# Two-block transformer kernel, first MoE: token rows fetched from DRAM by index and transposed, in place of a gather by matmul

## The reference, cut to what matters

```python
xf = h.reshape(b * t, d)                 # normed x, 256 x 1024
g_sel = argmax(xf @ w_rg + b_rg)         # one of 4 groups of 8 experts
top_v, top_i = lax.top_k(e_in_group, 2)  # two experts within the group
top_w = softmax(top_v) * g_w
combine = ...                            # 256 x 32, two non-zero weights in a row
for e in range(32):
    hid = silu(xf @ w_gate[e]) * (xf @ w_up[e])            # 1024 -> 128
    y = y + combine[:, e:e + 1] * (hid @ w_down[e])        # 128 -> 1024
```

## Time and profile before

| | |
|---|---|
| runs of the kernel before (us) | 1004.64, 997.33, 998.43; median 998.43 |
| the profiled execution: its time, its span (us) | 1000.59, 998.8 |
| PE busy, share of the span | 836.7 us, 84% |
| DVE, ACT, POOL busy | 244.0, 162.9, 56.1 us |
| moved by DMA | 307.33 MB, mean 308 GB/s |
| the chain that ended last | PE 61%, DMA 33% |

### The profile page before, as it was taken

The page is one execution under the profiler, slowest core; times in us unless marked ns, Lnnn a source line. Parts: engine busy times, 40 slices in busy tenths (PEclk is TensorE's granted clock), DMA queues, the critical chain, the costliest instruction groups (busy, mean ns, idle before and its releaser), DMA issues.

```text
span 998.8 us, 20766 instructions
## 1 busy us (share of the span) xinstructions
PE 836.7 (84%) x9275; PEld 579.0 (58%) x9275; DVE 244.0 (24%) x624; ACT 162.9 (16%) x347; POOL 56.1 (6%) x62
## 2 busy tenths in 40 slices
PE   7999999999899998999999888756657676676665
PEld 4656588885666674445665666544535454454543
DVE  2023830232422222135344412110202011020201
ACT  2012322330311114101553200000000000000000
POOL 8000300000011000061000000000000000000000
PEclk9999999999999999999799999888988888797977
DMA  9965524048478999244254899999999999999996
GB/s 255 380 218 216 209 107 169 1 184 321 169 275 323 410 402 381 97 160 168 85 204 156 323 422 413 429 430 425 427 428 430 430 427 427 427 430 430 428 427 262
DMA packets 53674, 307.33 MB, mean 308 GB/s; under 512 B 4584, under 2 KB 5824, under 8 KB 41344
## 3 DMA queue, kind: packets, MB, share of 16 engines
q1 hardware_dynamic: 50688, 301.85, 75.3%
q0 software_dynamic: 1760, 2.77, 1.1%
q10 hardware_dynamic: 1184, 2.10, 0.5%
HBM read 303.56 MB, written 3.15 MB: 307 GB/s over the span
## 4 chain that ended last, share of the span: by engine, by line
PE 61%; DMA 33%; DVE 2%; issue 1%; ACT 1%; SPq 0%; ACTq 0%; DVEq 0%
PE ps L1514 58%; DMA ring<-in_w_up 21%; DMA ring<-in_w_down 7%; DMA ring<-in_w_gate 5%; PE ps L1540 1%; DMA ring<-in_w_in 1%; PE ps L1680 1%; PE ps L1643 0%; PE ps L1568 0%; PE ps L1885 0%; ACT arena L814 0%; DVE xx L1285 0%; PE ps L1717 0%; PE ps L1829 0%; DVE arena L1236 0%
## 5 line engine op out<-in xcount | busy, mean ns | idle before, releaser
L1514 PE MATMUL ps<-ring,arena 128*32 128x128 f32 (+3 forms) x5968 | 288.1, 339 | 136.9 <-DMA ring<-in_w_gate 45.8
L1514 PEld LDWEIGHTS ps<-ring,arena 128*32 128x32 f32 (+1 forms) x5968 | 202.1, 125 | 221.4 <-issue 78.1
L1514 PE MATMUL ps<-ring,xx 128*128 128x512 f32 (+2 forms) x384 | 151.6, 553 | 0.0
L1514 PE MATMUL ps<-arena 32*128 32x256 f32 (+10 forms) x1216 | 130.8, 376 | 3.5 <-ACT arena L816 0.9
L1514 PEld LDWEIGHTS ps<-ring,xx 128*128 128x128 f32 x384 | 70.4, 192 | 75.7 <-issue 74.8
L1514 PEld LDWEIGHTS ps<-arena 32*128 32x128 f32 (+4 forms) x1216 | 82.6, 175 | 33.0 <-issue 25.4
L804 ACT ACTIVATE arena<-ps 128x128 f32<-128x128 f32 x40 | 11.1, 278 | 469.9 <-PE ps L1514 469.9
L1229 DVE TENSOR_TENSOR arena<-arena,ps 128x128 f32<-128x128 f32 x40 | 11.5, 288 | 293.6 <-ACT arena L804 293.6
L1514 PE MATMUL ps<-xx,ring 128*128 128x256 f32 (+2 forms) x400 | 78.9, 381 | 0.0
L1514 PEld LDWEIGHTS ps<-xx,ring 128*128 128x128 f32 (+2 forms) x400 | 63.6, 174 | 12.3 <-issue 1.5
L1514 PE MATMUL ps<-arena,xs 128*128 128x128 f32 x512 | 65.0, 288 | 1.9 <-DVE arena L1124 1.9
(11 more groups left out here) (266 smaller groups left out, 534.8 us busy)
## 6 DMA issues: line engine op xcount, KB each, us to landing
ring<-in_w_up SPq DMA_DIRECT2D x38, 2048.0 KB, 25.2
ring<-in_w_down SPq DMA_DIRECT2D x38, 2048.0 KB, 23.8
ring<-in_w_gate SPq DMA_DIRECT2D x37, 2048.0 KB, 23.6
ring<-in_w_in SPq DMA_DIRECT2D x15, 2048.0 KB, 18.5
ring<-in_w_out SPq DMA_DIRECT2D x4, 2048.0 KB, 8.0
arena<-in_w_gate SPq DMA_DIRECT2D x2, 2048.0 KB, 10.5
arena<-in_w_up SPq DMA_DIRECT2D x2, 2048.0 KB, 14.1
arena<-in_w_down SPq DMA_DIRECT2D x2, 2048.0 KB, 9.6
```

The costliest lines, as they stand in the source:

```text
L1514: ins = pe.matmul(dst, w, x, start=start, stop=stop, skip_group_check=True)
```

## The change: from the third group on, rows by indirect DMA

- ACT writes the normed x (`xs`, two tiles of 512 KB) to a new DRAM array, `normed_x_scratch`, as soon as it is computed.
- Groups 0 and 1 gather as before, with two `pick` buffers now in place of one. DVE writes `pick` of group n + 2 during group n, right behind the two multiplications by the gains.
- In each group n, 0 to 7, PE multiplies that `pick` by a column of token numbers (`slot_tokens`, two matmuls of one column, between the gate strips and the up strips). The result is the token number of each of the 128 slots of group n + 2. DVE copies it as an integer into `token`, behind `hidden`.
- POOL waits for it (`s_tok`) and issues an indirect DMA: 128 rows of 4 KB, the rows of `normed_x_scratch` that `token` names, into one of two buffers `xg_tm`. It does so eight times; the last two fetch the rows for groups 8 and 9, which only a further round would use. POOL's loads of `const2` and the clearing of `aug_l` and `aug_r` stand behind this loop.
- In groups 2 to 7 PE does not gather; it waits for the rows (`s_row`) and transposes them, eight transposes of 128 x 128, into the same banks.
- Ahead of the last scatter PE waits until all eight indirect DMAs have landed, since their buffers are used anew behind it.
- The semaphore of the weighted picks is a new one (`s_pw`), and PE's down strips now also wait for `s_tok`.

```diff
+        picks = [pick, kb3(15, TT, P)]
+        xg_tm = [kb(16, D), kb(20, D)]
...
+        xs_dram = nc.dram_tensor("normed_x_scratch", (T, D), F32).ap()
...
+            with pool.Fori(0, rounds) as r:
+                with pool.Fori(0, NGRP // 2) as g:
+                    for half in range(2):
+                        pool.wait_ge(s_tok, pool.snap(r * NGRP + g * 2 + (half + 1)))
+                        pool.sem_inc(s_seen, 1)
+                        pool.wait_ge(s_xd, 32)
+                        pool.indirect_dma_start(xg_tm[half], None, xs_dram,
+                                                bass.IndirectOffsetOnAxis(token[:, half:half + 1], 0)
+                                                ).then_inc(s_row[half], 16)
+                pool.wait_ge(s_rounds, 1)
+                pool.reg_load(rounds, nround[0:1, 0:1])
+
             pool.wait_ge(s_y[0], 2)
             pool.dma_start(const2, a["shape_const2"]).then_inc(s_const2, 16)
...
+                if m == 1:
+                    for tt in range(TT):
+                        act.wait_ge(s_xs, 3 + tt)
+                        act.dma_start(xs_dram[tt * P:(tt + 1) * P, :], xs[:, tt, :]).then_inc(s_xd, 16)
...
+                if b == 0:
+                    pick_slots(0, EG, 1)
...
-                def group(n, r, c_next):
+                def group(n, r, c_next, half):
                     gathered(n)
+                    dve.wait_ge(s_posm[0], dve.snap(r + 1))
+                    dve.wait_ge(s_pw, dve.snap(n + 1))
+                    pick_slots(0, dve.snap(c_next + EG), half)
                     hidden(dve.snap(n + 1), 0)
-                    next_picks(n, r, c_next)
+                    dve.tensor_copy(token[:, half:half + 1], bank(7, 1, T)).then_inc(s_tok, 1)
+                    dve.wait_ge(s_ptp[0], dve.snap(n + 1))
+                    weigh_slots(0, c_next, dve.snap(n + 2), 1 - half)
...
+                def gathered_rows(half, q):
+
+                    pe.wait_ge(s_row[half], pe.snap(q * 16))
+                    for k in range(KD):
+                        ins = pe.transpose(bank(6 + k // 4, P, (k % 4) * P), xg_tm[half][:, k * P:(k + 1) * P], ident)
...
+                def slot_tokens(n, half):
+
+                    pe.wait_ge(s_pick[0], val(n + 3))
+                    for tt in range(TT):
+                        mm(bank(7, 1, T), picks[half][:, tt, :], const[:, C_TOK + tt:C_TOK + tt + 1], tt == 0,
+                           tt == TT - 1)
...
-                    gather(n)
-                    pe.wait_ge(s_pick[0], val(n * 2 + 2))
+                    if isinstance(n, int):
+                        gather(n)
+                    else:
+                        gathered_rows(parity, q)
+                    pe.wait_ge(s_pw, n1)
...
                     for i in range(2):
                         arrived(c[i], q)
                         w4 = slot4(c[i])
+                        if i == 1:
+                            slot_tokens(n, parity)
...
                     arrived(c[2], q)
+                    pe.wait_ge(s_tok, n1)
                     pe.wait_ge(s_hid[0], n1)
...
                 if b == 0:
+                    for half in range(2):
+                        pe.wait_ge(s_row[half], pe.snap(pe.snap(rounds) * (16 * TURNS1)))
                     scatter(pe.snap(pe.snap(rounds) * NGRP + 1), last=True)
```

More of the change, by code:

```diff
@@ L142, in program @@
         stat = sb("stat", [P, 256])
-        posm = sb("posm", [P, TT, NE + EG])
+        posm = sb("posm", [P, TT, NE + 2 * EG])
+        token = sb("token", [P, 2], I32)
         comb = sb("comb", [P, TT, NE + EG])
@@ L329, in program @@
         s_pick = [sem(f"moe_picks{b}") for b in (0, 1)]
+        s_pw = sem("moe1_picks_weighed")
+        s_xd = sem("normed_x_in_dram")
+        s_tok = sem("slot_tokens")
+        s_seen = sem("slot_tokens_seen_by_pool")
+        s_row = [sem(f"slot_rows_loaded{i}") for i in (0, 1)]
         s_xgp = [sem(f"moe_gathered{b}") for b in (0, 1)]
@@ L1118, in group_columns, with pick_slots, weigh_slots @@
                 return slice(c0, c0 + EG) if isinstance(c0, int) else bass.ds(c0, EG)
-            def pick_slots(b, c0):
+            def pick_slots(b, c0, i=0):
                 shape = [P, TT, EG, SLOTS]
                 iota = const[:, C_IOTA:C_IOTA + SLOTS].unsqueeze(1).unsqueeze(1).broadcast_to(shape)
-                dve.tensor_tensor(pick.rearrange("p t (j s) -> p t j s", j=EG),
+                dve.tensor_tensor(picks[i].rearrange("p t (j s) -> p t j s", j=EG),
                                   posm[:, :, group_columns(c0)].unsqueeze(3).broadcast_to(shape), iota,
                                   ALU.is_equal).then_inc(s_pick[b], 1)
-            def weigh_slots(b, c0, picked):
+            def weigh_slots(b, c0, picked, i=0):
                 dve.wait_ge(s_pick[b], picked)
@@ L1142, in weigh_slots @@
                 dve.tensor_tensor(pick_w.rearrange("p t (j s) -> p t j s", j=EG),
-                                  pick.rearrange("p t (j s) -> p t j s", j=EG),
+                                  picks[i].rearrange("p t (j s) -> p t j s", j=EG),
                                   comb[:, :, group_columns(c0)].unsqueeze(3).broadcast_to(shape),
-                                  ALU.mult).then_inc(s_pick[b], 1)
+                                  ALU.mult).then_inc(s_pw, 1)
             def clear_route(b):
@@ L1274, in moe @@
                             for half in range(2):
-                                group(dve.snap(r * NGRP + g * 2 + half), r, dve.snap(g * (2 * EG) + (half + 1) * EG))
+                                group(dve.snap(r * NGRP + g * 2 + half), r, dve.snap(g * (2 * EG) + (half + 1) * EG),
+                                      half)
                         else:
                             group2(dve.snap(r * NGRP + g), r, dve.snap(g * EG + EG))
-                    dve.wait_ge(s_pick[b], dve.snap(r * (2 * NGRP) + (2 * NGRP + 2)))
+                    if b == 0:
+                        dve.wait_ge(s_pick[0], dve.snap(r * NGRP + (NGRP + 2)))
+                    else:
+                        dve.wait_ge(s_pick[1], dve.snap(r * (2 * NGRP) + (2 * NGRP + 2)))
                     dve.tensor_scalar(posm[:, :, :], posm[:, :, :], -float(SLOTS), None,
@@ L1805, in strips @@
                     return ins
+                def gathered_rows(half, q):
+                    pe.wait_ge(s_row[half], pe.snap(q * 16))
+                    for k in range(KD):
+                        ins = pe.transpose(bank(6 + k // 4, P, (k % 4) * P), xg_tm[half][:, k * P:(k + 1) * P], ident)
+                        if read[0]:
+                            ins.then_inc(s_used, read[0])
+                            read[0] = 0
+                        if k % 4 == 3:
+                            ins.then_inc(s_xgp[0], 1)
+                def slot_tokens(n, half):
[3 more added lines that the diff above has]
+                           tt == TT - 1)
                 def gather(n):
[L1809 removed]
+                    pe.wait_ge(s_pick[b], val(n + 1 if b == 0 else n * 2 + 1))
                     for half in range(2):
@@ L1813, in gather, with group @@
                             for tt in range(TT):
-                                ins = mm(bank(6 + half, P, i * P), xs[:, tt, k * P:(k + 1) * P], pick[:, tt, :],
+                                ins = mm(bank(6 + half, P, i * P), xs[:, tt, k * P:(k + 1) * P],
+                                         picks[n if b == 0 else 0][:, tt, :],
                                          tt == 0, tt == TT - 1)
                         ins.then_inc(s_xgp[b], 1)
-                def group(n, c, q):
+                def group(n, c, q, parity):
                     n1 = val(n + 1)
@@ L1910, in moe @@
                 if b == 0:
-                    group(0, FIRST1[0:3], 0)
-                    group(1, FIRST1[3:6], 0)
+                    group(0, FIRST1[0:3], 0, 0)
+                    group(1, FIRST1[3:6], 0, 1)
                 else:
@@ L1920, in moe @@
                             for half in range(2):
-                                group(pe.snap(r * NGRP + g * 2 + half), [s0 + 3 * half + n for n in range(3)], q)
+                                group(pe.snap(r * NGRP + g * 2 + half), [s0 + 3 * half + n for n in range(3)], q,
+                                      half)
                         else:
```

11 lines of the change are left out of this document (7 added, 4 removed).

## The result

| | before | after |
|---|---|---|
| median of 20 runs (us) | 1000.73 (997.33 to 1006.54) | 1006.88 (996.36 to 1014.04) |
| the profiled execution: its time, its span (us) | 1000.59, 998.8 | 1006.36, 1004.5 |

The ratio is 1.0051, interval [1.003, 1.0072]: the kernel is 5 to 6 us slower. The ratio goes by the fast runs and leaves out after's three slowest (1012.52 to 1014.04 us), while the medians take all twenty. The loss is less than the 1% I called the limit of no change, but the sign is wrong, and 1006.88 lies 1.9 us above my range of 991 to 1005. The forecast was 997.

A forecast was written before the change was run, and what follows sets the result against it. PE sets the first MoE's pace, with DMA weight loads close behind. PE's -17.0 + 7.2 us, less 7.6 taken back by late weights and 0.6 by the last rows, gives -1.6: 997 us from the median, range 991 to 1005.

The forecast's parts named there:

- the last rows: Before the last scatter: PE waits 0.6 us for fetched rows nobody reads; the scatter starts at 377.7 us.
- L: An indirect DMA's time from issue to landing, taken as 4.7 us for the last one; the gain is 6.3 - L.
- the first rival: Before the last scatter: the last rows land late, slower than before from 6.3 us to landing on; chance 0.28.
- a rival at 0.10: PE, waiting for weights, is granted its lower clock; costs 1 to 3 us in or behind the last group: 999; chance 0.10.
- the forecast stretch: First MoE, from the first gather's start to the last scatter's end: forecast 113.4 us, 115.04 before.
- PE, gather and token numbers: PE, first MoE: transposes replacing gathers save 17.0 us over six groups; token matmuls cost 7.2 over eight.
- The weights: SP's queue: starts 1.0 us earlier, five fetches add 6.4; last down weights at 374.3 us, taking back 7.6 of PE's gain.
- The down strips: PE, group 7: start as their weights land, 2.25 us earlier than before.
- The last scatter: PE, end of the first MoE: starts at 377.7 us instead of 379.34, with no slowing counted.
- three signs: Wrong if PE never waits for weights in groups 5-7, rows are waited for inside the loop, or 380 us gain vanishes by 550.
- The order of POOL: POOL: `const2`, clearing and small loads move behind the eighth fetch, done at about 385 us, cover over 30 us; costs nothing.
- The rival on bandwidth: Weight loads, first MoE: a second queue lets DMA reach 427 GB/s, gaining 2.7 us more, 994; chance 0.14.

The follow-up runs named there:

- quarter_rows: The changed kernel with each indirect fetch bringing 1 KB of each row instead of 4, reread by the transposes (another product): 995.26 us, ratio 0.9938.
- six_groups_const2_early: The changed kernel without the two spare fetches, with `const2`, the clearing and the small loads behind the second fetch: 1001.33 us, ratio 0.9997 against before.
- busy_wait: The changed kernel with 16 unused matmuls on PE ahead of its wait for the last rows: 1004.01 us, ratio 1.0027 against before.
- rows_in_four_groups: The changed kernel with fetched rows only in groups 2 to 5, no spare fetches, groups 6 and 7 gathering as before: 997.35 us, ratio 0.9973 against before.
- the two best: The changed kernel with rows in groups 2 to 4, or 2 to 5, `const2` behind the second fetch: 994.94 and 995.41 us, ratios 0.9952 and 0.995.
- before_again: The kernel before with only the loaded number of rounds held at 1 or more, run for a second trace: 1002.53 us, ratio 1.0012.
- no_spare_rows: The changed kernel without the fetches for groups 8 and 9 and the wait for them: 1000.17 us, ratio 1.0002 against before.
- two_groups: The changed kernel with fetched rows only in groups 2 and 3, `const2` and the small loads behind both fetches: 1000.49 us, ratio 0.9972 against before.
- four_groups_const2_early: The changed kernel with rows only in groups 2 to 5, no spare fetches, `const2` and small loads behind the second fetch: 995.41 us, ratio 0.995 against before.

## Why the prediction was wrong, by its own steps

The failed step is the last rows: "I take L = 4.7 ... The wait is 0.6 us". L was 7.0 us, and the wait 4.05. The gain was 6.3 - L by my own formula, so the deciding point was passed. I had this as the first rival, with 0.28. By that formula, though, L = 7.0 loses 0.7 us, and the stretch lost 5.0. The larger part is a second term, PE's lower clock behind a wait, which the sum had at nothing and a rival at 0.10: it cost 1.5 us in the last up strips and 2.5 in the last scatter. Of the 6.6 us between the forecast stretch and the measured one, L has 2.3, the clock 4.0.

1. **PE, gather and token numbers: right.** Eight transposes take 1.09 us (1.0). A group with all its weights takes 11.8 us (11.9). The token matmuls cost 0.67 (0.9): 0.61 of their own less what they overlap, gate and up strips together 4.37 instead of 3.70.
2. **The weights: right.** The last down weights, forecast at 374.3 us with the MoE at 267.97, thus at 380.5 with it at 274.19, landed at 380.4; the up weights at 375.3 (375.4). From the issue of group 4's gate weights to this landing it takes 72.1 us, 65.4 before: 6.7 us for five fetches, where a quarter of a load each gave 6.4. The size held; that it is all bytes, quarter_rows doesn't bear out. Also right was that the late weights take back most of PE's gain: PE idles 6.8 us for up weights in groups 6 and 7, each time longer than the 0.5 to 2.5 us I gave.
3. **The down strips: 1.5 us late.** I had them start as their weights land, 380.5. They start at 382.08, as the up strips ahead of them took 3.46 us instead of 1.95, at a granted clock of 0.60. I had put the lower clock at 0.10, said it would be hidden where weights bind, and left it out of the sum. In group 6 it is hidden: those 1.5 us only shorten the next wait. In group 7 the strips lie on the path. six_groups_const2_early has them at 1.96, and its down strips come with the weights.
4. **The last rows: failed.** They are asked for at 380.81 instead of 379.2, which is step 3 again and 0.1 more. L is 7.0, 2.3 more than I took. I had taken it from a plain load of the same size, with another behind it, and called it near since no indirect one had been seen. quarter_rows shows what that overlooks: with a quarter of the bytes the last fetch still takes 5.6 us. The second fetch of after shows it too: beside engines busy to 0.68 it took 5.4 us (4.3 in quarter_rows), where the plain load in an idle stretch took 3.4. The rest of L goes with the full engines: there whole rows took 7.0 to 8.3 us, more than the 1.28 us I had added. No run has a plain load alone in that place; `const2`, right behind the last fetch, took 8.8 us. So how much of L is owed to the rows being chosen by index stays open.
5. **The last scatter: not in the sum.** PE had idled 4.05 us, and the scatter took 6.21 us, 2.5 more than before. busy_wait shows this as the clock's, and as coming from the wait ahead of it.

From the forecast stretch, 113.4 us: +1.6 (asked for later), +2.3 (L), +0.2 (from the landing to the scatter), +2.5 (the slow scatter) gives 120.0; measured 120.07. Taking the last two fetches out and leaving `const2` early gives 112.67, 7.4 us less, and 0.7 us better than my forecast with a 0.6 us wait in it. The time of that kernel isn't below before's, though: 1001.33 us, ratio 0.9997 [0.9974, 1.002]. rows_in_four_groups has the same stretch, 112.69, and 0.9973 [0.9951, 0.9995]. So a gain of 2.4 us of stretch is at the edge of what these times show; the 4.1 and 4.2 us of the two best stand clear in both.

My range had a slip as well: its upper end of 1005 was to stand for an L near 11 us, but 6.3 - 11 gives a loss of 4.7 us and 1003.

Of the three signs that were to make the prediction wrong two didn't come: PE waited for weights in groups 6 and 7, and no rows were waited for inside the loop. The third, a gain at 380 us that is gone at 550, can't be read, as there was no gain. The profiled loss does shrink: after is 11.3 us late at the end of the last scatter, 7.9 at the second MoE's first gather and 5.7 at the end. The order of POOL, costed at nothing for the changed kernel, was costed rightly there; its ACT line 950, behind the wait, ran at 434.46 us, 160.3 from t0 (153.9 before), so with time to spare. The rival on bandwidth had nothing for it: 409 and 410 GB/s, as before.

The late start of the MoE in after, 6.22 us, lies wholly in the first block. By the matmuls that start at 103.26 us before and at 109.49 in after all of it is there, and PE's rows keep that distance up to t0; so ACT's new issues, at the MoE's start, have no part in it. Two pieces of PE's work show where more than half of it comes from, in before, then in after:

```profile
37.85 17.57 PE L1514 MATMUL ps<-ring,xx 128*128 128x8 f32 x64
...
87.88 14.00 PE L1514 MATMUL ps<-ring,xx 128*128 128x512 f32 x32
```

```profile
40.69 19.27 PE L1553 MATMUL ps<-ring,xx 128*128 128x8 f32 x64
...
92.41 15.70 PE L1553 MATMUL ps<-ring,xx 128*128 128x512 f32 x32
```

```profile
45.00:50.00 5.00, 5.00 (x9) 1.97 (x8) 0.51 (x2) 0.06 (x1) 0.00 (x0) 0.66 1.05 387
90.00:95.00 5.00, 5.00 (x14) 2.65 (x13) 1.64 (x6) 2.72 (x4) 0.00 (x0) 0.78 0.49 158
```

After is 2.84 us late before the first pair, in the first projection, and before_again is by 3.1 in the same place; each of the two stretches at a granted clock of 0.66 and 0.78, where before has 1.00, adds 1.70. What stays open is what starts these two stretches. Seven of the ten traces of kernels made from the changed one have them, the two of before don't, nor do no_spare_rows (which starts with before_again: 271.07, 271.04), two_groups and four_groups_const2_early. So they aren't tied to the change as such; that it makes them more likely is neither shown nor ruled out.

## What to carry to other kernels

A transfer that nobody reads still has a price if something waits for it, and most of all at the end of a stage, where no later work covers its time to landing; leave it out or move the wait. When a change makes an engine wait, price the wait and also the slower work right behind it: 1.1 to 2.7 us here for waits of 2.2 to 4.1 us. Once two resources are near their limit, shifting all of the work from one to the other turns the bound round: without spare rows and with `const2` early, six groups took 2.4 us off the stretch, three or four groups 4.2 and 4.1 us.

## What the runs showed of the hardware

- An indirect fetch of 128 rows of 4 KB takes POOL 0.94 to 1.04 us to issue and 5.4 to 8.3 us to land (after), of 1 KB 4.3 to 6.5 us (quarter_rows). It lands within that time beside a queue on SP whose own loads take 25 us (after, 25.2 and 26.0).
- In after, behind waits of 3.20 and 3.63 us the next 64 records of strips took 3.46 us instead of 1.95; behind one of 4.05 us eight matmuls took 6.21 instead of 3.67, behind one of 2.24 us in quarter_rows 5.37. The granted clock was 0.58, 0.60 and 0.50 in those of after. Behind waits of 0.71 us (six_groups_const2_early) and 1.63 us (no_spare_rows) the strips took 1.96 and 1.95, and where the wait was filled with matmuls the scatter took 3.67.
- 512 KB and four small loads on POOL's queue, placed among the weights, held one weight load back to 9.1 us behind the one before it in no_spare_rows, instead of 5.9 in after.
- Issues on SP took 0.37 us each before; in after those of group 7's up and down weights, at 349.26 and 355.16 us, took 5.73 and 4.79 us.
